# Latent attention's heads: rotation ahead of the norm, keys rotated once, and few-row products woven between the matmuls of gate chunks

## The chip, the cores and the metric

The kernel runs on one core of a Trainium2 chip. The metric is the device time in microseconds of one execution. TensorE (PE in the profile) multiplies, VectorE (DVE) and ScalarE (ACT) read its results from PSUM, GpSimd (POOL) does a few element-wise steps, and SyncE's queue (SP) loads the weights.

## The reference

Two transformer blocks of two layers each, all in float32, on 272 tokens (16 meta tokens and 256 others). The change is in the first block's latent attention, `mla`, which runs twice, once in each layer:

```
q = (rms_norm(c_q, q_a_g) @ w_uq).reshape(B, L, 8, 96)
kv = (rms_norm(c_kv, kv_a_g) @ w_ukv).reshape(B, L, 8, 128)
k_nope, v = kv[..., :64], kv[..., 64:]
k = concatenate([k_nope, broadcast(k_rope)], axis=-1)      # 64 + 32 = 96
q = rms_norm(q, q_norm_g);  k = rms_norm(k, k_norm_g)      # over the 96 of each head
q = concatenate([q[..., :64], apply_rope(q[..., 64:], cos, sin)], axis=-1)
k = concatenate([k[..., :64], apply_rope(k[..., 64:], cos, sin)], axis=-1)
o = causal_block_attention(q, k, v)
```

The last 32 rows of each key head are the same `k_rope` for all eight heads before the norm. The norm divides a head's 96 values at a token by one root, times a gain for each of the 96. `apply_rope` mixes row i with row i+16 of the 32, so it commutes with the division but not with the gain. The same layer has a gated recurrence (`hgrn2`) whose four heads are normed in the same way, and gates `sigmoid(h @ w_gate)` of 3 x 1024 columns.

## The kernel before, in words

Activations are held transposed: features on the 128 partitions, the 272 tokens along the free axis. Weights come as chunks of 128x1024 float32 (512 KB) through a ring of four slots that SP's queue fills in the order in which TensorE uses them. In the first block's projections TensorE uses a chunk as eight 128x128 weights against the activations (`project`); one float32 matmul is two instructions in the trace, here called passes.

PSUM has eight banks. `take` hands them out in strict rotation: each new product takes the next bank and waits until the engine that read the bank's result of eight takes ago has freed it. A product is therefore bound to the readers of the eight products before it.

The order of the work is a list of steps written out by hand (`schedule`). Each engine walks the same list and runs its own part of each step, if it has one; the instructions of one engine run in that order, so an engine stands still when the next step's input is late. Between engines there are semaphores and the banks.

The steps around the change, in each of the two layers, are these. `hgrn_values` makes the recurrence's outputs, `mla_up` multiplies up the queries (16 matmuls of 96 rows out), the keys (8 of 64 rows) and the values (3). Then there are three norms over heads, each in the same four parts: ACT squares the heads into the tile `SQ`; TensorE sums each head's rows with a matmul whose weight is a column of ones placed at the head's own output row (`row_sums`: 4 or 8 output rows); ACT takes the square root and DVE the reciprocal of these 4 or 8 rows (tile `HR`, part of `RS`; semaphore `row_roots`); TensorE spreads each row over 128 or 96 partitions with a matmul that has only 4 or 8 input rows (`spread`: one bank for each head), and DVE multiplies the head by it and by the gain. The three norms are that of the recurrence (`hgrn_norm`, `hgrn_spread`), of the queries (`head_norm`/`head_spread` with 0) and of the keys (with 1). After the heads' norm DVE rotates all eight heads' last 32 rows in four instructions: a shuffle, two products and a sum (`head_spread`). Between these steps stand six of the eight chunks of gate 2 (`gate(l, 2, m)`), which depend on nothing in them. After them comes the attention head by head.

HN is the normed input, CST the constants, MU and RS two scratch tiles, GATE the gates' tiles, and `region` holds all the rest, the heads among them.

Of the kernel before, what the change touches and what calls it, by code (L numbers as in the profile page):

```python
# [162 lines left out]
def parameters(i):  # L163
# [9 lines left out]
    col = lambda v: np.asarray(v).reshape(-1, 128).T  # L173
    for l in range(DEPTH):
# [7 lines left out]
        put(f"qn{l}", i["q_norm_g"][l][:, None])  # L182
        put(f"kn{l}", i["k_norm_g"][l][:, None])
# [8 lines left out]
        put(f"rbias{l}", np.concatenate([i["moe_br_g_2"][l], i["moe_br_e_2"][l].reshape(-1)])[None])  # L192
    put("ibias", i["ab_gate_b_2"][0, :4][:, None])
# [156 lines left out]
def build_program(nc, stream, params, consts, x_in, out, scratch):  # L350
    n_chunks = stream.shape[0] // 128
    with ExitStack() as ctx:
# [168 lines left out]
        def _(pe):  # L521
# [50 lines left out]
            def project(key, x, n=T, chunks=1, ready=None):  # L572

                dst, done = take(*key)
                for c in range(chunks):
# [129 lines left out]
            def row_sums(key, x, rows, heads):  # L705

                dst, done = take(*key)
                for h in range(heads):
                    mm(dst[:heads, :T], cst("pick", 15 - h, heads, rows), x(h), h == 0, h == heads - 1, done if h == heads - 1 else None)

# [5 lines left out]
            def hgrn_norm(l):  # L716
                pe.wait_ge(sem("hgrn_squares"), l + 1)
                row_sums(("hgrn_var", l), sq, 128, 4)

            def hgrn_spread(l):  # L720
                pe.wait_ge(sem("row_roots"), 3 * l + 1)
                for h in range(4):
                    spread(("hgrn_root", l, h), h, 128, 4)

# [6 lines left out]
            def mla_up(l):  # L731
                pe.wait_ge(sem("latents"), 2 * l + 1)
                for g in range(2):
                    w = chunk()
                    for h in range(4):
                        dst, done = take("q", l, 4 * g + h)
                        for k in range(2):
                            mm(dst[:QK, :T], w[:, 192 * h + 96 * k : 192 * h + 96 * k + 96], CQ[:, k, :], k == 0, k == 1, done if k else None)
                pe.wait_ge(sem("latents"), 2 * l + 2)
# [8 lines left out]
            def head_norm(l, which):  # L748
                pe.wait_ge(sem("head_squares"), 2 * l + which + 1)
                row_sums(("head_var", l, which), lambda h: SQ[:QK, T * h : T * h + T], QK, HEADS)  # L750

            def head_spread(l, which):
                pe.wait_ge(sem("row_roots"), 3 * l + 2 + which)
                for h in range(HEADS):
                    spread(("head_root", l, which, h), h, QK, HEADS)

            def att_scores(l, h):
                if h == 0:
                    pe.wait_ge(sem("heads_ready"), 2 * l + 2)
# [427 lines left out]
        def _(act):  # L1187
# [131 lines left out]
            def mla_up(l):  # L1319
                for h in range(HEADS):  # L1320
                    evacuate(("q", l, h), QH[:QK, h, :], rows=QK)
                fn(KH[NOPE:QK, :, :], bc(KR[NOPE:QK, None, :], [ROPE, HEADS, T]), ACT.Copy)
# [5 lines left out]
            def head_norm(l, which):  # L1328
# [3 lines left out]
                fn(SQ[:QK, : HEADS * T], src, ACT.Square, sem("head_squares"))  # L1332

# [253 lines left out]
        def _(dve):  # L1587
# [198 lines left out]

            def head_spread(l, which):
                x = (QH, KH)[which]
                for h in range(HEADS):
# [3 lines left out]

                r = slice(NOPE, QK)
                half = ROPE // 2
                shape = [ROPE, HEADS, T]
                c, s = CONSTS["cos"][0], CONSTS["sin"][0]
                lane(nc.vector.stream_shuffle(RSQ[r, :, :], x[r, :, :], [(i + half) % ROPE for i in range(ROPE)]))
                tt(RSQ[r, :, :], RSQ[r, :, :], bc(CST[r, None, s : s + T], shape), ALU.mult)
                tt(x[r, :, :], x[r, :, :], bc(CST[r, None, c : c + T], shape), ALU.mult)  # L1800
                tt(x[r, :, :], x[r, :, :], RSQ[r, :, :], ALU.add, sem("heads_ready"))
# [546 lines left out]
def schedule():  # L2348

    s = [("norm", 0), ("start",), ("store_bias",)]  # L2350
    for l in range(DEPTH):
# [68 lines left out]
```

## Time and profile before

| | us |
|---|---|
| median of three runs (lowest, highest) | 2438.68 (2435.79, 2441.68) |
| the profiled execution, whole | 2439.65 |
| its span, first to last instruction | 2437.9 |
| busy: PE, DVE, ACT, POOL | 2276.0, 1509.6, 1074.8, 240.7 |
| the stage of the change in layer 0: start of gate 2's chunk 0 to start of the first scores | 58.49 |
| the same in layer 1 | 57.84 |
| mean granted TensorE clock over the execution | 0.955 |

The granted clock is 1.00 at 2.4 GHz and 0.50 at 1.2 GHz; a number between is a mean over a stretch with both. A time in the tables of the trace is counted from the start of the span. A row's "x16" counts instructions, so that eight float32 matmuls are x16.

### The profile page before, as it was taken

Reading aid. Unit: us, or ns where it says so; the run is one execution under the profiler, and the core shown is the slowest. Engines: PE = TensorE matmul, PEld = TensorE weight load, DVE = VectorE, ACT = ScalarE, POOL = GpSimd, SP = SyncE. Lnnn points to the kernel's source line nnn. Section 1 sums busy time; section 2 is a strip of 40 time slices with the busy share of each in tenths; the row PEclk is TensorE's granted clock in tenths of the full one; section 3 lists DMA queues with packets and bytes.
Section 4 is the critical chain, followed back from the end, with each engine's and each line's share of the span. In section 5 each row is a group of like instructions: output and inputs, shape, how many; then the busy total and the mean of one; then the engine's idle time right before and its main releaser. Section 6 shows DMA issues by size and latency. Waiting matters only on the chain.

```text
span 2437.9 us, 36698 instructions
## 1 busy us (share of the span) xinstructions
PE 2276.0 (93%) x13888; PEld 1888.5 (77%) x13888; DVE 1509.6 (62%) x2343; ACT 1074.8 (44%) x1530; POOL 240.7 (10%) x241
## 2 busy tenths in 40 slices
PE   8999999999999999999999789999999787999997
PEld 6678567899867856889977379887888476988786
DVE  2846265656294626576534566888775166788876
ACT  1142432434114243244432345766654265567665
POOL 2814000101091400010100000000000000000000
PEclk9999799999999989999999689999999898999999
DMA  4332123455333212355542135888865413688884
GB/s 159 129 121 79 44 69 130 147 178 170 129 130 115 86 52 70 130 175 179 188 142 96 35 119 194 297 297 304 302 215 166 146 44 110 218 305 297 309 297 140
DMA packets 109808, 396.86 MB, mean 163 GB/s; under 512 B 12088, under 2 KB 14144, under 8 KB 109376
## 3 DMA queue, kind: packets, MB, share of 16 engines
q1 hardware_dynamic: 108576, 393.45, 47.9%
q8 instruction: 111, 1.82, 0.3%
q10 hardware_dynamic: 1056, 1.06, 0.1%
q14 instruction: 65, 0.53, 0.1%
HBM read 393.40 MB, written 1.06 MB: 162 GB/s over the span
## 4 chain that ended last, share of the span: by engine, by line
PE 76%; DVE 16%; ACT 4%; issue 2%; DMA 2%; SPq 0%; DVEq 0%; ACTq 0%
PE psum L536 75%; DVE W_LO L1593 3%; DVE region L1598 2%; PE psum L544 1%; DMA ring<-in_weights 1%; DVE region L1601 1%; ACT region L1201 1%; DVE RS L1630 1%; DVE region L1605 1%; ACT W_HI L1196 1%; DVE SQ L1598 1%; ACT SQ L1201 1%; ACT L1205 1%; DVE X_LO L1598 1%; ACT L1201 0%
## 5 line engine op out<-in xcount | busy, mean ns | idle before, releaser
L1593 DVE TENSOR_TENSOR W_LO<-ring,W_HI 128x1024 fp32r<-128x1024 f32 x434 | 531.8, 1225 | 219.1 <-ACT W_HI L1196 208.5
L1196 ACT ACTIVATE W_HI<-ring 128x1024 fp32r<-128x1024 f32 x434 | 460.8, 1062 | 339.1 <-PE psum L536 243.0
L536 PE MATMUL psum<-HN,ring 128*128 128x272 f32 (+1 forms) x1600 | 383.1, 400 | 12.2 <-DVE HN L1605 12.2
L536 PEld LDWEIGHTS psum<-HN,ring 128*128 128x128 f32 x1600 | 309.2, 195 | 80.7 <-issue 20.4
L536 PE MATMUL psum<-X_HI,W_HI 128*128 128x256 f32 x800 | 230.1, 288 | 12.5 <-DVE W_LO L1593 9.7
L536 PE MATMUL psum<-X_LO,W_HI 128*128 128x256 f32 x800 | 224.9, 281 | 0.0
L536 PE MATMUL psum<-X_HI,W_LO 128*128 128x256 f32 x800 | 224.7, 281 | 0.0
L1205 ACT ACTIVATE region<-psum 128x272 f32<-128x272 f32 (+9 forms) x227 | 89.5, 394 | 284.1 <-PE psum L536 264.5
L1593 DVE TENSOR_TENSOR W_LO<-SQ,W_HI 128x1024 fp32r<-128x1024 f32 x128 | 156.9, 1225 | 37.4 <-ACT W_HI L1196 32.9
L536 PE MATMUL psum<-FN_HI,W_HI 128*128 128x272 f32 (+1 forms) x592 | 169.8, 287 | 0.0
L536 PE MATMUL psum<-W_HI,XG_HI 128*128 128x512 f32 x384 | 152.9, 398 | 17.3 <-DVE W_LO L1593 15.3
L536 PE MATMUL psum<-FN_LO,W_HI 128*128 128x272 f32 (+1 forms) x592 | 168.5, 285 | 0.0
L536 PE MATMUL psum<-FN_HI,W_LO 128*128 128x272 f32 (+1 forms) x592 | 168.4, 284 | 0.0
L536 PEld LDWEIGHTS psum<-X_HI,W_HI 128*128 128x128 f32 x800 | 152.6, 191 | 18.8 <-issue 9.4
L1196 ACT ACTIVATE W_HI<-SQ 128x1024 fp32r<-128x1024 f32 x128 | 136.0, 1062 | 68.3 <-PE psum L536 65.8
L536 PE MATMUL psum<-region 128*32 128x4 f32 (+12 forms) x1360 | 150.3, 254 | 7.2 <-ACT region L1205 5.1
L536 PEld LDWEIGHTS psum<-X_LO,W_HI 128*128 128x128 f32 x800 | 152.5, 191 | 1.8
L536 PEld LDWEIGHTS psum<-X_HI,W_LO 128*128 128x128 f32 x800 | 153.0, 191 | 0.0
L536 PE MATMUL psum<-W_HI,XG_LO 128*128 128x512 f32 x384 | 151.0, 393 | 0.0
L536 PE MATMUL psum<-W_LO,XG_HI 128*128 128x512 f32 x384 | 150.6, 392 | 0.0
L536 PE MATMUL psum<-F_HI,W_HI 128*128 128x272 f32 (+1 forms) x512 | 145.7, 285 | 0.0
L536 PE MATMUL psum<-F_LO,W_HI 128*128 128x272 f32 (+1 forms) x512 | 144.6, 282 | 0.0
(306 smaller groups left out, 4273.9 us busy)
## 6 DMA issues: line engine op xcount, KB each, us to landing
ring<-in_weights SPq DMA_DIRECT2D x615, 512.0 KB, 4.2
SQ<-in_weights SPq DMA_DIRECT2D x128, 512.0 KB, 4.9
XT<-in_x SPq DMA_DIRECT2D x1, 1088.0 KB, 5.0
CST<-in_consts SPq DMA_DIRECT2D x1, 1082.5 KB, 7.2
SQ<-bias_by_distance ACTq DMA_DIRECT2D x1, 1024.0 KB, 5.4
out<-XT SPq DMA_DIRECT2D x8, 128.0 KB, 1.9
PAR<-in_params SPq DMA_DIRECT2D x1, 572.0 KB, 8.1
bias_by_distance<-MIX ACTq DMA_DIRECT2D x1, 12.0 KB
```

What stands on the lines that cost most here:

```text
L536: ins = nc.tensor.matmul(dst, w, x, start=start, stop=stop, skip_group_check=True)
L544: ins = nc.tensor.transpose(dst, src, ident(k))
L1196: lane(nc.scalar.activation(W_HI[:, s % SPLIT, :], ring_slot(n), ACT.Copy), split_hi)
L1201: lane(nc.scalar.activation(dst, src, f, **kw), sem_)
L1205: nc.scalar.activation(dst, src, f, **kw).then_inc(banks.freed(key), 1)
L1593: lane(nc.vector.tensor_tensor(W_LO[:, s % SPLIT, :], ring_slot(n), W_HI[:, s % SPLIT, :].bitcast(F32), ALU.subtract), split_lo)
L1598: lane(nc.vector.tensor_tensor(dst, a, b, op), done)
L1601: ins = nc.vector.tensor_scalar(dst, a, s1, s2, op0) if op1 is None else nc.vector.tensor_scalar(dst, a, s1, s2, op0, op1)
L1605: lane(nc.vector.scalar_tensor_tensor(dst, a, s, b, op0, op1), done)
L1630: lane(nc.vector.reciprocal(ap, ap))
```

## The change

The arithmetic is the same up to its order. These things change:

1. The rotation comes ahead of the norm. The gain of the 32 rotated rows goes into the rotation: one product takes the shuffled rows times the shuffled gain times the sine, another the rows times the gain times the cosine (`turn_queries`, `turned_queries`; `scalar_tensor_tensor` in place of `tensor_tensor`). The gain vectors of the norm have ones there. The squares are still taken of the unrotated rows, so ACT's squares come between.
2. The keys' 32 rows are rotated once, in the rope's own 32x272 tile (`hgrn_values` on DVE), and copied to the eight heads by ACT (`turned_key_rows`) after the squares; the copy of the unrotated rows (`key_rows`) stays, for the squares.
3. `mla_up` is cut into `mla_q` and `mla_kv`, with the recurrence's row sums (`hgrn_norm`) between them.
4. The spreads and the heads' row sums are no longer steps of their own on TensorE: `project` takes a generator (`beside`) and runs its products between the matmuls of a gate chunk. Chunk 0 holds the recurrence's 4 spreads and the queries' 8 row sums, chunk 2 five spreads of the queries, chunk 3 the other three and the keys' 8 row sums, chunk 5 six spreads of the keys; the last two stand behind it (`last_heads`). Chunks 1 and 4 are plain.
5. The first scores no longer wait for a whole stage of DVE (`heads_ready`): head h's scores wait until DVE has normed key head h.

The diff, cut to its core (`head_squares` and `turned_key_rows` are ACT's, the three below them DVE's):

```diff
-            def project(key, x, n=T, chunks=1, ready=None):
+            def project(key, x, n=T, chunks=1, ready=None, beside=None, count=0):
...
                         mm(dst[:, :n], columns(w, 128 * k, 128), x(8 * c + k), c + k == 0, last, done if last else None)
+                        while given < count * (k + 1) // KT:
+                            next(beside)
+                            given += 1
...
             def gate(l, b, m):
                 at = first_column(l)
-                project(("gate", l, b, m), lambda k: HN[:, k, at:], T - at)
+                count = {0: 12, 2: 5, 3: 11, 5: 6}.get(m, 0) if b == 2 else 0
+                project(("gate", l, b, m), lambda k: HN[:, k, at:], T - at, beside=beside_gate(l, m), count=count)
+
+            def beside_gate(l, m):
+                if m == 0:
+                    yield from hgrn_spreads(l)
+                    yield from head_norms(l, 0)
+                elif m == 2:
+                    yield from head_spreads(l, 0, 0, 5)
+                elif m == 3:
+                    yield from head_spreads(l, 0, 5, HEADS)
+                    yield from head_norms(l, 1)
+                elif m == 5:
+                    yield from head_spreads(l, 1, 0, 6)
...
             def att_scores(l, h):
-                if h == 0:
-                    pe.wait_ge(sem("heads_ready"), 2 * l + 2)
+                banks.await_read(pe, ("head_root", l, 1, h))
...
-            def head_norm(l, which):
+            def head_squares(l, which):
                 src = (QH, KH)[which][:QK, :, :].rearrange("p h t -> p (h t)")
                 if which:
                     wait_bank("head_var", l, 0)
                 fn(SQ[:QK, : HEADS * T], src, ACT.Square, sem("head_squares"))
+
+            def turned_key_rows(l):
+                act.wait_ge(sem("key_turned"), l + 1)
+                fn(KH[NOPE:QK, :, :], bc(MU[NOPE:QK, None, :T], [ROPE, HEADS, T]), ACT.Copy, sem("keys_turned"))
...
+            def hgrn_values(l):
+                r = slice(NOPE, QK)
+                banks.await_read(dve, ("rope", l))
+                lane(nc.vector.stream_shuffle(MU[r, :T], KR[r, :], half_turned))
+                stt(MU[r, :T], MU[r, :T], turn_gain(l, 1, 1), SIN, ALU.mult, ALU.mult)
+                stt(RS[r, :T], KR[r, :], turn_gain(l, 1, 0), COS, ALU.mult, ALU.mult)
+                tt(MU[r, :T], MU[r, :T], RS[r, :T], ALU.add, sem("key_turned"))
+
+            def turn_queries(l):
+                r = slice(NOPE, QK)
+                banks.await_read(dve, ("q", l, HEADS - 1))
+                lane(nc.vector.stream_shuffle(RSQ[r, :, :], QH[r, :, :], half_turned))
+                stt(RSQ[r, :, :], RSQ[r, :, :], turn_gain(l, 0, 1), bc(SIN[:, None, :], [ROPE, HEADS, T]), ALU.mult, ALU.mult)
+
+            def turned_queries(l):
+                r = slice(NOPE, QK)
+                dve.wait_ge(sem("head_squares"), 2 * l + 1)
+                stt(QH[r, :, :], QH[r, :, :], turn_gain(l, 0, 0), bc(COS[:, None, :], [ROPE, HEADS, T]), ALU.mult, ALU.mult)
+                tt(QH[r, :, :], QH[r, :, :], RSQ[r, :, :], ALU.add)
...
-        s += [("hgrn_values", l), ("mla_up", l), ("hgrn_norm", l), ("gate", l, 2, 0), ("hgrn_gates", l), ("hgrn_spread", l), ("head_norm", l, 0)]
-        s += [("gate", l, 2, 1), ("head_spread", l, 0), ("head_norm", l, 1), ("gate", l, 2, 2), ("head_spread", l, 1)]
-        s += [("gate", l, 2, m) for m in range(3, 6)] + [("att_scores", l, 0), ("att_scores", l, 1), ("gate", l, 2, 6), ("gate", l, 2, 7)]
+        s += [("hgrn_values", l), ("mla_q", l), ("hgrn_norm", l), ("turn_queries", l), ("mla_kv", l), ("head_squares", l, 0), ("key_rows", l)]
+        s += [("hgrn_spread", l), ("turned_queries", l), ("head_norm", l, 0), ("head_squares", l, 1), ("turned_key_rows", l)]
+        s += [("gate", l, 2, 0), ("hgrn_gates", l), ("gate", l, 2, 1), ("gate", l, 2, 2), ("head_spread", l, 0), ("head_norm", l, 1)]
+        s += [("gate", l, 2, 3), ("gate", l, 2, 4), ("gate", l, 2, 5), ("last_heads", l), ("head_spread", l, 1)]
+        s += [("att_scores", l, 0), ("att_scores", l, 1), ("gate", l, 2, 6), ("gate", l, 2, 7)]
```

TensorE's order in layer 0 before, from the last row sums of the recurrence to the first scores (HN,ring is a gate chunk, SQ,CST are row sums, RS,CST are spreads, region the scores; x8 counts matmuls):

```order
L536 MATMUL psum<-SQ,CST 4x272 x4
L536 MATMUL psum<-HN,ring 128x272 x8
L536 MATMUL psum<-RS,CST 128x272 x4
L536 MATMUL psum<-SQ,CST 8x272 x8
L536 MATMUL psum<-HN,ring 128x272 x8
L536 MATMUL psum<-RS,CST 96x272 x8
L536 MATMUL psum<-SQ,CST 8x272 x8
L536 MATMUL psum<-HN,ring 128x272 x8
L536 MATMUL psum<-RS,CST 96x272 x8
L536 MATMUL psum<-HN,ring 128x272 x24
L536 MATMUL psum<-region 128x128
```

The same place now, from the end of chunk 0 through the plain chunk 1 into chunk 2:

```order
L541 MATMUL psum<-SQ,CST 8x272
L541 MATMUL psum<-HN,ring 128x272
L541 MATMUL psum<-SQ,CST 8x272 x2
L541 MATMUL psum<-HN,ring 128x272 x10
L541 MATMUL psum<-RS,CST 96x272
L541 MATMUL psum<-HN,ring 128x272 x2
L541 MATMUL psum<-RS,CST 96x272
L541 MATMUL psum<-HN,ring 128x272
L541 MATMUL psum<-RS,CST 96x272
```

The groups of four and eight are gone; a spread or a row sum stands between single matmuls of a gate, and ten of the gate's own (chunk 1 and the first two of chunk 2) separate the queries' last row sum from their first spread.

ACT's order in layer 0 now, from the recurrence's root (RS<-psum 4x272) to the keys' root (the second RS<-psum 8x272):

```order
L1238 ACT_TABLE_LOAD
L1238 ACTIVATE RS<-psum,CST 4x272
L1238 ACTIVATE region<-psum 64x272 x8
L1238 ACTIVATE region<-psum 128x512 x2
L1238 ACTIVATE region<-psum 16x512
L1234 ACTIVATE SQ<-region 96x2176
L1234 ACTIVATE region<-region 32x2176
L1238 ACTIVATE RS<-psum,CST 8x272
L1234 ACTIVATE SQ<-region 96x2176
L1234 ACTIVATE region<-MU 32x2176
L1238 ACT_TABLE_LOAD
L1238 ACTIVATE GATE<-psum 128x272
```

Before, the first 8-row root and both squares stood behind the gate's sigmoids, each with a table load of its own around it; now both squares and the keys' two copies stand ahead of the sigmoid of gate 2's chunk 0.

## Rows read from the trace of the kernel before

**Rows 1.** The page: chain that ended last by engine; weight DMAs

```profile
PE 76%; DVE 16%; ACT 4%; issue 2%; DMA 2%; SPq 0%; DVEq 0%; ACTq 0%
...
ring<-in_weights SPq DMA_DIRECT2D x615, 512.0 KB, 4.2
```

**Rows 2.** Timeline of PE, layer 0: start us, us, engine, line, operation [idle before]

```profile
270.16 2.95 PE L536 MATMUL psum<-ring,region 128*128 128x512 f32 x6
...
274.87 3.93 PE L536 MATMUL psum<-HN,ring 128*128 128x272 f32 x16
278.79 2.09 PE L536 MATMUL psum<-RS,CST 4*128 4x272 f32 x8
284.75 7.01 PE L536 MATMUL psum<-SQ,CST 96*8 96x272 f32 x16 [3.86 <-ACT SQ L1201]
291.69 3.93 PE L536 MATMUL psum<-HN,ring 128*128 128x272 f32 x16
295.63 5.24 PE L536 MATMUL psum<-RS,CST 8*96 8x272 f32 x16
300.80 5.82 PE L536 MATMUL psum<-SQ,CST 96*8 96x272 f32 x16
306.55 3.94 PE L536 MATMUL psum<-HN,ring 128*128 128x272 f32 x16
313.41 5.94 PE L536 MATMUL psum<-RS,CST 8*96 8x272 f32 x16 [2.92 <-DVE RS L1785]
319.28 14.24 PE L536 MATMUL psum<-HN,ring 128*128 128x272 f32 x48
333.36 2.80 PE L536 MATMUL psum<-region 96*128 96x128 f32 x12
```

**Rows 3.** Windows: stretch, us, PE PEld DVE ACT POOL busy, granted clock, DMA

```profile
274.87:333.36 58.49, 51.70 (x169) 31.59 (x169) 36.87 (x37) 17.17 (x17) 0.00 (x0) 0.77 0.19 63
883.64:941.48 57.84, 51.69 (x169) 31.98 (x169) 36.84 (x37) 16.99 (x17) 0.00 (x0) 0.76 0.19 63
298.20:304.60 6.40, 6.40 (x15) 2.32 (x15) 5.32 (x8) 1.26 (x1) 0.00 (x0) 0.50 0.00 0
...
867.61:878.90 11.29, 11.29 (x49) 7.24 (x48) 0.00 (x0) 7.75 (x14) 0.00 (x0) 1.00 0.28 93
...
916.25:919.97 3.72, 3.72 (x17) 2.95 (x16) 3.69 (x2) 1.76 (x2) 0.00 (x0) 1.00 0.46 141
```

**Rows 4.** Timeline of ACT, layer 0

```profile
266.94 2.01 ACT L1201 ACTIVATE region<-region 32x2176 f32<-32x2176 f32 x1
268.98 5.22 ACT L1205 ACTIVATE region<-psum 64x272 f32<-64x272 f32 x11
...
276.32 0.48 ACT L1205 ACTIVATE RS<-psum,CST 4x272 f32<-4x272 f32 x1
278.91 1.28 ACT L1205 ACT_TABLE_LOAD   x1 [2.11 <-PE psum L536]
280.20 0.40 ACT L1205 ACTIVATE GATE<-psum 128x272 f32<-128x272 f32 x1
...
282.68 2.02 ACT L1201 ACTIVATE SQ<-region 96x2176 f32<-96x2176 f32 x1
```

**Rows 5.** Timeline of DVE, layer 0

```profile
279.62 0.44 DVE L1773 TENSOR_TENSOR region<-psum,region 128x272 f32<-128x272 f32 x1 [0.88 <-PE psum L536]
280.09 0.50 DVE L1605 SCALAR_TENSOR_TENSOR region<-region,PAR 128x272 f32<-128x272 f32 x1
...
301.54 2.58 DVE L1798 STREAM_SHUFFLE region<-region 32x2176 f32<-32x2176 f32 x1
...
309.06 2.42 DVE L1598 TENSOR_TENSOR region<-region 32x2176 f32<-32x2176 f32 x1
311.51 1.84 DVE L1785 RECIPROCAL RS<-RS 8x272 f32<-8x272 f32 x1
```

More of the change, by code:

```diff
@@ L173, in parameters @@
     col = lambda v: np.asarray(v).reshape(-1, 128).T
+    turns = [None, None]
     for l in range(DEPTH):
@@ L181, in parameters @@
         put(f"kva{l}", col(i["kv_a_norm_g"][l]))
-        put(f"qn{l}", i["q_norm_g"][l][:, None])
-        put(f"kn{l}", i["k_norm_g"][l][:, None])
+        for c, name in enumerate(("q", "k")):
+            g = np.asarray(i[f"{name}_norm_g"][l], np.float32)
+            put(f"{name}n{l}", np.concatenate([g[:NOPE], np.ones(ROPE)])[:, None])
+            turns[c] = g[NOPE:], np.roll(g[NOPE:], ROPE // 2)
         put(f"lb{l}", col(i["hgrn_lb_logits"][l]))
@@ L192, in parameters @@
         put(f"rbias{l}", np.concatenate([i["moe_br_g_2"][l], i["moe_br_e_2"][l].reshape(-1)])[None])
+        at = PARAMS[f"rbias{l}"][0]
+        out[NOPE:QK, at : at + 4] = np.stack([turns[0][0], turns[0][1], turns[1][0], turns[1][1]], axis=1)
     put("ibias", i["ab_gate_b_2"][0, :4][:, None])
@@ L668, in gate, with last_heads @@
                 at = first_column(l)
-                project(("gate", l, b, m), lambda k: HN[:, k, at:], T - at)
+                count = {0: 12, 2: 5, 3: 11, 5: 6}.get(m, 0) if b == 2 else 0
[11 more added lines that the diff above has]
+                    yield from head_spreads(l, 1, 0, 6)
+            def last_heads(l):
+                for _ in head_spreads(l, 1, 6, HEADS):
+                    pass
             def branch_out(l, b, c):
@@ L717, in hgrn_norm, with hgrn_spreads @@
                 pe.wait_ge(sem("hgrn_squares"), l + 1)
-                row_sums(("hgrn_var", l), sq, 128, 4)
-            def hgrn_spread(l):
+                for _ in row_sums(("hgrn_var", l), sq, 128, 4):
+                    pass
+            def hgrn_spreads(l):
                 pe.wait_ge(sem("row_roots"), 3 * l + 1)
@@ L723, in hgrn_spread @@
                     spread(("hgrn_root", l, h), h, 128, 4)
+                    yield
             def mla_norm(l):
@@ L729, in mla_norm, with mla_q @@
                 column_sums(("ckv_var", l), lambda k: sq(6), 1, T)
-            def mla_up(l):
+            def mla_q(l):
                 pe.wait_ge(sem("latents"), 2 * l + 1)
@@ L746, in mla_up, with head_norms, head_spreads @@
                     mm(dst[:n, :], CKV[:, lo : lo + n], w[:, 512:1024], done=done)
-            def head_norm(l, which):
+            def head_norms(l, which):
                 pe.wait_ge(sem("head_squares"), 2 * l + which + 1)
[L750 to L754, printed above, removed]
+                yield from row_sums(("head_var", l, which), lambda h: SQ[:QK, T * h : T * h + T], QK, HEADS)
+            def head_spreads(l, which, lo, hi):
+                if lo == 0:
+                    pe.wait_ge(sem("row_roots"), 3 * l + 2 + which)
+                for h in range(lo, hi):
                     spread(("head_root", l, which, h), h, QK, HEADS)
+                    yield
             def att_scores(l, h):
-                if h == 0:
-                    pe.wait_ge(sem("heads_ready"), 2 * l + 2)
+                banks.await_read(pe, ("head_root", l, 1, h))
                 for i, (lo, n) in enumerate(TOK1):
@@ L1317, in mla_norm, with mla_q, mla_kv @@
                 root(("ckv_var", l), MU[:, :T], T, 128)
-            def mla_up(l):
+            def mla_q(l):
                 for h in range(HEADS):
                     evacuate(("q", l, h), QH[:QK, h, :], rows=QK)
-                fn(KH[NOPE:QK, :, :], bc(KR[NOPE:QK, None, :], [ROPE, HEADS, T]), ACT.Copy)
+            def mla_kv(l):
                 for h in range(HEADS):
@@ L1332, in head_norm, with key_rows @@
                 fn(SQ[:QK, : HEADS * T], src, ACT.Square, sem("head_squares"))
+            def key_rows(l):
+                fn(KH[NOPE:QK, :, :], bc(KR[NOPE:QK, None, :], [ROPE, HEADS, T]), ACT.Copy)
+            def turned_key_rows(l):
+                act.wait_ge(sem("key_turned"), l + 1)
+                fn(KH[NOPE:QK, :, :], bc(MU[NOPE:QK, None, :T], [ROPE, HEADS, T]), ACT.Copy, sem("keys_turned"))
+            def head_norm(l, which):
                 wait_bank(*(("head_root", l, 0, HEADS - 1) if which else ("hgrn_root", l, 3)))
@@ L1785, in head_norm, with turn_gain @@
                 lane(nc.vector.reciprocal(HR[:HEADS, :], HR[:HEADS, :]), sem("row_roots"))
+            def turn_gain(l, which, shuffled):
+                at = PARAMS[f"rbias{l}"][0] + 2 * which + shuffled
+                return PAR[NOPE:QK, at : at + 1]
+            half_turned = [(i + ROPE // 2) % ROPE for i in range(ROPE)]
+            COS, SIN = (CST[NOPE:QK, CONSTS[n][0] : CONSTS[n][0] + T] for n in ("cos", "sin"))
+            def hgrn_values(l):
[15 more added lines that the diff above has]
+                tt(QH[r, :, :], QH[r, :, :], RSQ[r, :, :], ALU.add)
             def head_spread(l, which):
                 x = (QH, KH)[which]
+                if which:
+                    dve.wait_ge(sem("keys_turned"), l + 1)
                 for h in range(HEADS):
@@ L1792, in head_spread @@
                     free(ins, "head_root", l, which, h)
[L1794 to L1801, printed above, removed]
             def att_scores(l, h):
```

4 lines of the change are left out of this document (3 added, 1 removed).

## The prediction

> **What bounds the kernel now.** I read the chain of waits first: three quarters of it is TensorE at work [rows 1]. A microsecond taken from TensorE's own path is a microsecond of the end, and ring and DMA are no other bound here. Then I read TensorE's timeline through the stage that the change touches, from gate 2's chunk 0 to the first scores, once in each layer [rows 2], and then the same stretches as windows with the granted clock [rows 3]. Three things are to be seen there.
>
> The stage takes 58.49 us in layer 0 and 57.84 in layer 1 [rows 3]. TensorE is busy for 51.70 and 51.69 of these, so it stands idle for 6.79 and 6.15 us. In layer 0 that is 3.86 us ahead of the queries' row sums, which wait for ACT's squares, and 2.92 ahead of the keys' spreads, which wait for a reciprocal that DVE reaches only after the queries' rotation [rows 2].
>
> The work is slower than it need be. A gate chunk takes 3.93 us in one place (16 passes, 0.246 each), but the three plain ones at 319.28 take 14.24 in place of 11.8. Eight row sums take 7.01 and 5.82, eight spreads 5.24 and 5.94 [rows 2]. In layer 1, 48 passes of the up-projection with 96 and 64 rows out run at clock 1.00 in 11.29 us, 0.235 each [rows 3], so 16 passes could take 3.8.
>
> The cause is the clock: its mean over the stage is 0.77 and 0.76 [rows 3]. In layer 0 it falls to 1.2 GHz in the middle of the queries' spreads, with TensorE never idle: from 298.20 to 304.60 TensorE is busy for all 6.40 us at 0.50 [rows 3]. What the engine did before it fell was a gate chunk and some 2.5 us of products with only eight input rows; it came back in the middle of the row sums, which have 96 input rows. So here the spreads, though busy, are what loses the clock, and gates or row sums are what gets it back.
>
> The Trainium skill ("TensorE: Matmul & The Clock Gate", part 1 on the clock gate) ties the clock to how busy TensorE is and warns of idle gaps. The 6.40 busy microseconds at 0.50 [rows 3] speak against that as the whole rule. By the page alone weaving would give back no clock, since the products keep TensorE just as busy where they stand now; that result is the second rival below.
>
> **The change part by part.** TensorE does the same 168 passes in the stage: 96 of six gate chunks, 8 of the recurrence's spreads, 64 of heads' row sums and spreads. The recurrence's row sums only change places with the keys and values ahead of the stage, so the stage starts at the same time.
>
> *The passes at 2.4 GHz.* Layer 0: 6 x 3.93 = 23.58 for gates, 2.09 for the recurrence's spreads [rows 2], 64 x 0.235 = 15.04; together 40.7. Layer 1 has 256 columns in gates: 6 x 3.72 = 22.32 [rows 3], together 39.45. No row shows single few-row passes between single gate passes. If the exchange costs TensorE nothing, 40.7 stands; the upper bound would be a small gap at each change of kind. The recurrence's four spreads, each with its own bank and wait, ran at 0.26 a pass against 0.235 for longer runs [rows 2, 3], and 0.025 on 72 passes is 1.8 us a layer. I take nothing, as 16 passes of a gate directly behind other work show no gap.
>
> *The waits that go.* Count from the start of chunk 0. The recurrence's row sums now end before keys (8 matmuls, 16 x 0.235 = 3.8) and values (2.95, rows 2), that is 6.7 us before. ACT's table load and root take 1.28 + 0.48, DVE's reciprocal 1.84 [rows 4, 5], so the recurrence's roots are there at -3.1, and TensorE asks at +0.5. ACT then moves keys and values (5.22) and squares the queries (2.02, rows 4): -4.9 + 7.2 = +2.3. TensorE asks for the squares after four gate matmuls and four spreads, 1.96 + 2.09 = +4.05. Both waits are covered, with 3.6 and 1.7 us to spare.
>
> *The wait that comes.* Banks go round in eights. Chunk 0 takes one, then four spreads, one row-sum bank, chunk 1, chunk 2: the queries' first spread in chunk 2 is the ninth and needs the bank of chunk 0, which ACT frees with the gate's sigmoid. From the end of the queries' row sums ACT has the root 0.48, the keys' squares 2.02, the copy of the turned rows 2.01, a table load 1.28 and the sigmoid 0.40 [rows 4]: 6.2, with hand-over 6.3. TensorE has chunk 1 and two matmuls of chunk 2: 3.93 + 0.98 = 4.9 in layer 0, 3.72 + 0.93 = 4.65 in layer 1. New waits: 1.4 and 1.65 us. Behind the waiting spread stand the other six matmuls of chunk 2 and everything after.
>
> By the Trainium skill ("ScalarE: Activation LUTs", What ACT_TABLE_LOAD costs) a switch of tables costs a drain of about 1.38 us on top of the load; the sigmoid here starts 0.01 us after the load's 1.28 [rows 4], so the row decides. With the page's drain this wait would be 1.4 us longer in each layer, 2.8 in all.
>
> DVE is no later: from the roots at -3.1 + 0 it shuffles and multiplies the queries (2.58 + about 2.5) until +2.1, waits for the recurrence's spreads, multiplies 4 x (0.44 + 0.50) until about +6.2, finishes the rotation (2.5 + 2.42) at +11.2 and, with the row sums done at 3.93 + 2.09 + 3.76 = +9.8, gives the reciprocal at +13.1 [rows 5]. TensorE asks at +14.7, the bank comes at +16.1. That a 32x2176 product with a gain costs about what one without does (2.42) is an estimate; 0.50 against 0.44 on 272 columns [rows 5] bounds it by 2.75, which the 3 us to the bank hold.
>
> *The keys.* Their squares are done 2.5 us after the queries' sums and are asked for over 10 later. After their row sums (end of chunk 3) ACT has load and root (1.76) and DVE the reciprocal (1.84): 3.6, against chunk 4 and one matmul of chunk 5, 4.4: covered by 0.8, in layer 1 by 0.6. The rotation of all key heads (2.58 + three products of about 2.43, 9.9 us of DVE) becomes four instructions on 272 columns; before, it was hidden under the three gates [rows 2], so its removal is worth nothing directly. ACT's copy of 2.01 is the price, and it is in the wait above. The first scores ask for one key head; DVE norms a head in 0.5 us, at the pace of the spreads.
>
> *Weights.* A chunk lands 4.2 us after issue [rows 1]; a woven chunk takes over 6 us and a plain one 3.9 with three others ahead in the ring. No new wait.
>
> *The clock.* In the new order full-row work is everywhere between spreads, but not by much: in chunk 2 there are 5 x 0.47 = 2.35 us of spreads beside 3.93 of gate and the new wait of 1.4; around the end of chunk 5 eight spreads (3.8) beside 3.93. No row shows such a mixture. From below, the clock stays at 2.4 GHz: cost 0. From above, both places lose it as the spreads did: the spreads of rows 2 were 1.4 and 2.1 us over 3.8, the row sums behind 2.0 over, the three gates behind 2.4, so a fall costs 3.4 to 4.5, and two of them about 8 a layer. I take one fall a layer, 4 us, the middle.
>
> *Sum.* Layer 0: 40.7 + 1.4 + 4 = 46.1, a gain of 58.49 - 46.1 = 12.4. Layer 1: 39.45 + 1.65 + 4 = 45.1, a gain of 12.7. Together 25.1 us. The attention that follows is unchanged and starts earlier; nothing later is bound by a fixed time. The profiled execution took 2439.65, so 2414.6; it lies 1 us above the median of the runs, so 2414 in round numbers.
>
> **Rivals.** *A, full clock.* As above with no fall: 58.49 - 42.1 = 16.4 and 57.84 - 41.1 = 16.7, together 33: 2406 to 2407, less 1 against the median. For it: every gate chunk that stands between two few-row groups runs at its full 3.93 [rows 2], so gate work holds the clock. Against it: in chunk 2 the new wait and the spreads come together.
>
> *B, only the waits.* The few-row passes and the gates beside them run at the mean pace they have now, 51.7 us in both layers, and only idle time changes: 6.79 - 1.4 and 6.15 - 1.65, together 9.9: 2430, 2429 against the median. For it: 51.7 twice, in two different places of the program. Against: the long groups of spreads that came before each fall are gone.
>
> *C, the clock is lost for the whole stage.* With a spread every second or third matmul TensorE may never do enough full work to get the clock back once it is gone. At 1.2 GHz 16 passes take 7.01 [rows 2], 0.44 each: 168 x 0.44 = 73.9 against 58.49, and 57.84, that is 31 us slower: 2470. It decides where over half of the passes are slow: the stage now spends 58.49 / 168 = 0.348 a pass, between 0.242 and 0.44, so slower from 54% on. Against it: row sums brought the clock back at 304.6, and chunks 1 and 4 are plain.
>
> *D, the weave stands still.* Every woven product holds the gate's matmuls behind it. If one of the covered waits (1.7 us at the squares, 0.6 to 0.8 at the keys' roots) is missed in each chunk by as much as it has now, TensorE is idle for as long as before and the falls stay: no change, 2438.
>
> **How the numbers follow.** Forecast, about one fall a layer: 0.48, 2414. A: 0.27. B: 0.15. C: 0.04. D: 0.06. The range reaches down to A with the 1 us of the median and a little more, 2404, and up into B, 2427. No change means within 0.2%, about 5 us, which is what three runs can tell. Faster 0.91 (forecast, A, B and a part of D), within 0.2% 0.05, slower 0.04 (C).
>
> **What would show it.** Right: the stage, gate 2's chunk 0 to the first scores, takes 42 to 48 us in both layers, its mean clock is 0.85 or more, and TensorE's longest idle time in it is 1.2 to 2 us at the first spread of chunk 2, behind ACT's gate sigmoid. No wait stands at chunk 0's spreads or row sums nor at chunk 5. Wrong in the clock: passes woven in chunks 2, 3 or 5 at 0.44, a mean clock under 0.80. Wrong in the waits: idle time in chunk 0 or 5, or DVE as the releaser in chunk 2. And wrong in the whole: attention's first part, or the recurrence ahead, longer by what the stage gained.

## The result and the profile after

| | before | after |
|---|---|---|
| median (lowest to highest) | 2440.18 (2435.79 to 2443.39), 4 runs | 2463.79 (2455.31 to 2473.70), 4 runs |
| ratio to before, 95% interval | | 1.0107 [1.0079, 1.0135] |
| the profiled execution, whole | 2439.65 | 2459.64 |
| stage of the change, layer 0 | 58.49 | 69.80 |
| stage of the change, layer 1 | 57.84 | 62.61 |

The changed kernel is 1.1% slower, where 1% faster was forecast. First the windows of the changed kernel: the two stages (they answer to the first two of [rows 3]), then two stretches inside them (us, busy PE PEld DVE ACT POOL, granted clock, DMA).

```profile
274.68:344.48 69.80, 68.04 (x170) 29.20 (x169) 22.18 (x28) 17.85 (x17) 0.00 (x0) 0.69 0.16 53
902.15:964.76 62.61, 60.59 (x169) 27.36 (x168) 21.86 (x28) 17.66 (x17) 0.00 (x0) 0.75 0.18 59
...
300.80:324.70 23.90, 23.90 (x44) 8.32 (x44) 2.96 (x6) 0.40 (x1) 0.00 (x0) 0.51 0.06 22
921.90:952.80 30.90, 30.90 (x59) 11.14 (x59) 3.45 (x7) 2.04 (x4) 0.00 (x0) 0.51 0.05 17
```

The idle time has gone, as intended: 1.76 and 2.02 us are left of 6.79 and 6.15. What went up is TensorE's busy time for the same passes, 51.7 to 68.0 and 60.6 us. The mean clock is 0.69 and 0.75, under the 0.77 and 0.76 of before. The last two rows say that TensorE can be busy for every microsecond of 24 and of 31 and still run at 1.2 GHz.

The timeline of TensorE in layer 0 answers to [rows 2].

```profile
274.68 0.73 PE L541 MATMUL psum<-HN,ring 128*128 128x272 f32 x2
275.33 0.72 PE L541 MATMUL psum<-RS,CST 4*128 4x272 f32 x2
275.98 0.73 PE L541 MATMUL psum<-HN,ring 128*128 128x272 f32 x2
276.64 1.18 PE L541 MATMUL psum<-RS,CST 4*128 4x272 f32 x4
...
291.17 4.85 PE L541 MATMUL psum<-HN,ring 128*128 128x272 f32 x20
297.79 0.66 PE L541 MATMUL psum<-RS,CST 8*96 8x272 f32 x2 [1.76 <-ACT GATE L1238]
...
306.58 1.22 PE L541 MATMUL psum<-RS,CST 8*96 8x272 f32 x2
307.73 1.28 PE L541 MATMUL psum<-HN,ring 128*128 128x272 f32 x2
308.94 1.22 PE L541 MATMUL psum<-RS,CST 8*96 8x272 f32 x2
...
332.14 0.73 PE L541 MATMUL psum<-HN,ring 128*128 128x272 f32 x2
...
333.42 0.73 PE L541 MATMUL psum<-HN,ring 128*128 128x272 f32 x2
...
344.48 5.27 PE L541 MATMUL psum<-region 96*128 96x128 f32 x12
349.68 8.60 PE L541 MATMUL psum<-HN,ring 128*128 128x272 f32 x32
```

Read starts, since the ends of matmuls overlap. At the full clock a gate matmul (x2) between spreads takes 275.33 - 274.68 = 0.65 us; sixteen passes in 3.93 are 0.49 for one matmul [rows 2], and that row holds the two ends of its block (e2 will show 0.46 without them). Two spreads in a row take 1.11 (276.64 to 277.75), so the second adds only 0.46, although it too has a bank of its own: the gap comes with the change of kind, not with each product. The row of weight loads says what the gap is:

```profile
275.33 0.29 PEld L541 LDWEIGHTS psum<-RS,CST 4*128 4x128 f32 x2 [0.36 <-issue]
275.98 0.30 PEld L541 LDWEIGHTS psum<-HN,ring 128*128 128x128 f32 x2 [0.36 <-issue]
```

The loads of a new kind start together with its first matmul (275.33 and 275.98 in both timelines), 0.36 us after the last load: none is laid beside the matmul ahead. A pair of a gate matmul and a spread takes 1.28 us at the full clock (332.14 to 333.42) and 2.36 at the low one (306.58 to 308.94). The clock is low from 280 to 290.7, from 300.8 to 324.7 and from 334.8 to 351.8 (windows of 0.52, 0.51 and 0.50); the last of these also slows the first scores (5.27 against 2.80) and the two gate chunks behind them (8.60 against 7.60).

The two stages lost 11.31 and 4.77 us and what stands behind the first one 3.5: 19.6 of the 20.0 between the profiled executions.

### The profile page after: what moved, and what is told of

Its sections match the earlier page's. It is cut to its first block, busy times and chain, and to the rows that moved or that the text cites. A ratio compares the mean times of both kernels' runs of the same rounds, so it can differ in the third digit from the quotient of the medians.

```text
span 2457.8 us, 36718 instructions
## 1 busy us (share of the span) xinstructions
PE 2306.3 (94%) x13888; PEld 1886.3 (77%) x13888; DVE 1494.5 (61%) x2343; ACT 1074.0 (44%) x1528; POOL 240.3 (10%) x241
## 4 chain that ended last, share of the span: by engine, by line
PE 78%; DVE 15%; ACT 4%; issue 2%; DMA 1%; DVEq 0%; ACTq 0%; SPq 0%
PE psum L541 76%; DVE W_LO L1636 3%; DVE region L1641 1%; PE psum L549 1%; DVE region L1644 1%; ACT region L1234 1%; DVE RS L1673 1%; DVE region L1648 1%; DVE X_LO L1641 1%; DVE SQ L1641 1%; ACT SQ L1234 1%; ACT W_HI L1229 1%; ACT L1238 0%; ACT L1234 0%; DMA ring<-in_weights 0%
## 5 line engine op out<-in xcount | busy, mean ns | idle before, releaser
L541 PE MATMUL psum<-HN,ring 128*128 128x272 f32 (+1 forms) x1600 | 407.6, 411 | 12.2 <-DVE HN L1648 12.2
L541 PEld LDWEIGHTS psum<-region 128*32 128x32 f32 (+6 forms) x1360 | 107.8, 144 | 50.1 <-issue 26.4
```

The lines of the kernel that those rows point to most:

```text
L541: ins = nc.tensor.matmul(dst, w, x, start=start, stop=stop, skip_group_check=True)
```

## Experiments

Two explanations stood at the start. *S, the change of shape*: each exchange between a gate's 128x128 weight and a few-row one costs a gap. *W, the wait*: the new wait in chunk 2 is what takes the clock. For the low clock itself a third: *F, the few-row spreads*, with 4 or 8 input rows, take it, waits or not. Beside them the kernel before was timed again: its medians were 2437.58 (beside e1 to e4), 2438.24 (e5 to e8) and 2438.25 (e9 to e12). Ratios therefore compare better across these groups than medians do.

| kernel | median us | ratio to before |
|---|---|---|
| changed kernel | 2463.79 | 1.0107 [1.0079, 1.0135] |
| e1, products in blocks | 2417.61 | 0.9925 [0.9897, 0.9953] |
| e2, woven, spreads of full shape | 2411.42 | 0.9901 [0.9869, 0.9933] |
| e3, woven, all of full shape | 2429.75 | 0.9968 [0.9948, 0.9988] |
| e4, before with spreads of full shape | 2434.70 | 0.9994 [0.9977, 1.0010] |
| e5, the wait hidden | 2457.97 | 1.0077 [1.0052, 1.0101] |
| e6, blocks and spreads of full shape | 2401.25 | 0.9849 [0.9827, 0.9870] |

**e1, blocks instead of the weave.** The same steps, banks and order of steps; a chunk's few-row products stand in one block behind its eight gate matmuls.

```diff
-                        while given < count * (k + 1) // KT:
-                            next(beside)
-                            given += 1
+                for _ in range(count):
+                    next(beside)
```

> The changed kernel, but each gate chunk's few-row products stand behind its eight matmuls and not between them; the rotation, the cut of the up-projection and the order of all else stay. Theory S (two costs of weaving: each change between a gate matmul and a few-row product exposes a weight load, 0.15 us at 2.4 GHz and 0.3 at 1.2, and the clock, once lost, does not come back among them): the changes of kind fall from some 40 to 8 in a layer, the stage from 69.8 and 62.6 us to about 52, total about 2427. Rival W (the new wait at the bank of chunk 0 and the longer chain through ACT are the cost): the weave is innocent, the total stays near 2460.

Measured 2417.61, under the 2427 expected. Windows of e1's stages and its timeline in layer 0:

```profile
276.49:319.54 43.05, 43.05 (x170) 27.68 (x169) 22.14 (x28) 17.86 (x17) 0.00 (x0) 0.93 0.26 86
875.20:914.33 39.13, 39.13 (x169) 26.85 (x169) 21.71 (x28) 17.79 (x18) 0.00 (x0) 1.00 0.28 94
```

```profile
282.38 5.52 PE L541 MATMUL psum<-SQ,CST 96*8 96x272 f32 x16
...
314.52 5.09 PE L541 MATMUL psum<-RS,CST 8*96 8x272 f32 x16
319.54 5.27 PE L541 MATMUL psum<-region 96*128 96x128 f32 x12
```

TensorE is never idle, since the block comes late enough for the bank. Layer 1 runs at 1.00 and takes 39.13 us. So the weave itself, not the rest of the change, made it slow. The clock still falls in layer 0, in row sums behind spreads and at the last spreads, and it is low in the first scores of both layers (5.27 and 5.22 in place of 2.80).

**e2, spreads of full shape, still woven.** The 4 or 8 input rows become 128; the added ones are multiplied by zero. The heads' spreads also get 128 output columns in place of 96.

```diff
-                mm(dst[:rows, :T], ident(heads)[:, row : row + 1].to_broadcast([heads, rows]), HR[:heads, :], done=done)
+                mm(dst[:, :T], ident(128)[:, row : row + 1].to_broadcast([128, 128]), RS[:, :T], done=done)
```

> The changed kernel, woven as it is, but every spread reads 128 rows (weight: 128x128 from the identity, zero against all rows but one) and writes 128, so that its shape is a gate matmul's; the row sums keep 96 rows in and 8 out. Theory S, in the form that the shape is what costs: no gap at spreads, still 0.15 us at each change to and from the row sums, and the clock no longer falls at the spreads: stage about 46, total about 2415. Rival B (the gap belongs to the change of PSUM bank, whatever the shape): a gate matmul beside a spread still takes 0.65 us, total above 2430. Rival R (only the share of input rows counts for the clock, nothing for the gap): gap 0.65, clock 1.00, total about 2425.

Measured 2411.42, with both waits still there. Windows of the stages, then TensorE's timeline in layer 0:

```profile
274.79:318.64 43.85, 42.09 (x169) 26.99 (x169) 21.70 (x28) 17.85 (x17) 0.00 (x0) 1.00 0.25 84
870.40:915.30 44.90, 42.88 (x170) 28.14 (x169) 22.14 (x29) 17.92 (x18) 0.00 (x0) 0.96 0.25 82
```

```profile
275.81 0.62 PE L541 MATMUL psum<-HN,ring 128*128 128x272 f32 x2
276.27 1.08 PE L541 MATMUL psum<-RS,CST 128*128 128x272 f32 x4
277.19 0.62 PE L541 MATMUL psum<-HN,ring 128*128 128x272 f32 x2
...
283.76 0.73 PE L541 MATMUL psum<-HN,ring 128*128 128x272 f32 x2
284.42 1.08 PE L541 MATMUL psum<-SQ,CST 96*8 96x272 f32 x4
...
292.05 0.70 PE L541 MATMUL psum<-RS,CST 128*128 128x272 f32 x2 [1.76 <-ACT GATE L1238]
```

```profile
275.58 0.42 PEld L541 LDWEIGHTS psum<-HN,ring 128*128 128x128 f32 x2
```

Between full-shape products a step is 0.46 us and the gap is gone: the weight of the gate matmul at 275.81 is loaded from 275.58 (last row, weight loads), ahead of its start. At the row sums, which keep 8 output columns, a gate matmul still takes 0.66. The clock is 1.00 through all of layer 0, with a wait of 1.76 in its middle, and the long low stretches are gone from layer 1 too. W is right only in small: after layer 1's wait of 2.02 the clock is low for about 3 us (0.54 from 888 to 891) and then comes back, in the same weave. In chunk 0 the two kernels differ in nothing but the spreads' input rows, and there the changed kernel lost its clock at 280. It did so in layer 0 only: in layer 1 the same chunk ran at 1.00. The mean clock of each whole run says the same as the profiles: 0.963 to 0.967 in the four runs of e2, 0.942 to 0.951 in the four of the changed kernel. The row sums woven among gates (96 input rows) do not take the clock here, although the gap stands at them. That speaks for F, and against the gaps or few output columns as what takes it. e4 parts F from the gaps once more, since inside its blocks there is no gap to remove.

**e3, the row sums too.** Their weight comes from a new table of constants, a one in column 15 of 143.

```diff
+    put("wide", np.tile(np.eye(143)[15], (96, 1)))
...
-                    mm(dst[:heads, :T], cst("pick", 15 - h, heads, rows), x(h), ...)
+                    mm(dst[:, :T], cst("wide", 15 - h, 128), x(h), ...)
```

> As the woven kernel with 128-row spreads, and the heads' row sums have full weights too (128 rows, of which 96 are not zero, by 128 columns), so that every product in the stage has the shape of a gate matmul. Theory S: no gap anywhere, 168 passes of 0.246 us and the one wait: stage 43 in layer 0, 41.5 in layer 1, total about 2408. Rival B: the gaps stay, 0.65 us for a single gate matmul, total above 2430.

The gaps are gone, as S says. Timeline of TensorE in layer 1, whose stage starts at 876.90; its only wait, then the first scores:

```profile
892.65 0.70 PE L542 MATMUL psum<-RS,CST 128*128 128x272 f32 x2 [2.22 <-ACT GATE L1242]
...
916.68 2.80 PE L542 MATMUL psum<-region 96*128 96x128 f32 x12
```

The stage takes 39.78 us at a clock of 1.00, of which the passes are 37.56. Layer 0 takes 42.49 with 40.53 busy, but its clock is low for some 3 us after the wait of 1.96 (0.54 from 291.3 to 294.9). In layer 1 no low clock followed a longer wait, 2.22. So what a wait of about 2 us does to the clock is not settled by its length in these runs. The whole got slower than e2 all the same, 2429.75 where 2408 was expected. The loss is spread over the program outside the stage; e7 to e12 follow it.

**e4, the kernel before with e2's edit alone.**

> The kernel before, with nothing changed but the spreads, which read and write 128 rows. Theory S: the clock no longer falls in the spreads, but it still falls at the idle time ahead of the queries' row sums, and all waits stay: stage about 50, total 2439 - 15 = about 2424. Rival: the number of input rows has nothing to do with the clock, it falls as before, and wider weights cost a little: 2440 to 2445.

A miss. Timeline of e4 in layer 0:

```profile
295.13 3.93 PE L536 MATMUL psum<-RS,CST 128*128 128x272 f32 x16
299.02 3.83 PE L536 MATMUL psum<-SQ,CST 96*8 96x272 f32 x16
...
312.08 6.70 PE L536 MATMUL psum<-RS,CST 128*128 128x272 f32 x16 [5.36 <-DVE RS L1785]
```

The same block of sixteen passes, with no gap inside it before or now, no longer takes the clock, and the row sums behind it keep it (3.93 and 3.83 against 5.24 and 5.82 in [rows 2]): F holds. But TensorE only arrives earlier at the reciprocal behind DVE's rotation: the wait grew from 2.92 to 5.36, the clock fell in it (0.81 from 309 to 312), and the time is that of before within its interval. The stage took 54.99, not 50.

**e5, the wait hidden.** Woven with the shapes of the changed kernel, but the five spreads of chunk 2 begin in its second half.

```diff
+                        share = max(k - 3, 0) / 4 if count == 5 else (k + 1) / KT
-                        while given < count * (k + 1) // KT:
+                        while given < int(count * share):
```

> The woven kernel with one edit: the five spreads of a chunk that has five start in its second half (none beside k = 0 to 3), so that ACT's gate sigmoid is over when the first of them asks for a bank; all shapes are as in the changed kernel. If the wait of 1.8 to 2.0 us in the third chunk is what loses the clock: no wait longer than 0.5 us there, the second layer's mean clock back near 1.00, its stage at 46 to 50 us where the changed kernel has 62.6. If it is the mixture of few-row products among gate matmuls that doesn't keep the clock (rival): the wait goes, the clock falls at the same place or a chunk later, and the second layer's stage stays at 57 to 62 us; the whole within 8 us of the changed kernel's 2464.

The wait is 0.40 us in layer 0. In chunk 0 of layer 0 the clock held this time. In chunk 2 it falls all the same, after five microseconds of mixture (timelines of both layers):

```profile
294.57 0.66 PE L541 MATMUL psum<-RS,CST 8*96 8x272 f32 x2 [0.40 <-ACT GATE L1239]
...
299.46 1.22 PE L541 MATMUL psum<-HN,ring 128*128 128x272 f32 x2
...
900.37 0.66 PE L541 MATMUL psum<-RS,CST 4*128 4x272 f32 x1
900.95 1.22 PE L541 MATMUL psum<-HN,ring 128*128 128x256 f32 x2
```

In layer 1 it fell in chunk 0, where TensorE had waited for nothing. That stage takes 61.81 us at 0.72 (896.36 to 958.17). As the cause of the long low stretches W is out. Hiding the wait was worth 6 us of medians, of which the waits are 3.4; the intervals of the two ratios overlap. The few-row weave lost its clock in every stage of the two kernels that have it, but not at the same place: first in chunk 0 of layer 0 and in chunk 2 of layer 1 in the changed kernel, and the other way round in e5. What decides between them was not found.

**e6, both edits that helped.**

> The changed kernel with both edits that helped singly: the products of a chunk as one block behind its gate matmuls, and the spreads as full 128 by 128 products. If the two losses (the change of shape at each exchange, and few-row products that leave the clock low) are separate and nothing else changes: stages of 41 to 43 us in both layers, few changes of shape left, the whole at 2404 to 2410, under each of the two alone (2417.6 and 2411.4). If woven full-row spreads had already taken all there was (rival): no better than 2411, within 0.2%.

```profile
279.31:318.51 39.20, 39.20 (x170) 28.50 (x170) 21.43 (x27) 17.86 (x17) 0.00 (x0) 1.00 0.28 94
870.67:908.59 37.92, 37.92 (x170) 28.50 (x170) 21.45 (x27) 17.68 (x17) 0.00 (x0) 1.00 0.29 97
```

The stages, 39.20 and 37.92 us, and the whole are below what was expected. Both run without idle time at 1.00, and the first scores behind layer 0 take 2.80 again. With 2401.25 it beats both kernels: 1.5% under before and, by the ratios, 2.6% under the changed one. All of the change but the weave is in it. Its gain over e4 is 33 us for the same spreads. The new order of rotation and norms and the place of the blocks have it between them; e4's idle time is what they remove, but no run parts them.

**e7 and e8, the table.** e7 is e3 with a table of 160 columns. e8 is e2 with the table of 143 loaded and used by nothing.

> Woven with all side products in full 128 by 128 shape, as in the run of 2429.75, but the added table of constants has 160 columns (640 bytes a partition) in place of 143 (572). If the loss of that run outside the stage (its later stages each ran a little longer) comes from where the wider table pushes the buffers behind it: 2408 to 2413, the late row sums at 0.46 us each. If it comes from the row sums' shape or from the table's load: 2427 to 2432 again.

> The version with full-row spreads alone (2411.42) and an unused table of constants of 143 columns in front of the buffers; every instruction is the same. If the place of the buffers is the cause: 2426 to 2432. If the shape of the row sums is: 2409 to 2414.

e7 2426.75, ratio 0.9968 [0.9947, 0.9989]; e8 2435.40, ratio 0.9988 [0.9970, 1.0006]. An unused table costs 24 us by the medians and 21 by the ratios: the row sums' shape is not to blame for e3. It is more than the 2426 to 2432 expected for the place. A width of 640 bytes does not mend it; e7 alone, inside neither range but next to the second, would have pointed at the wrong cause.

**e9 and e10, which side of the shape.** Row sums with 128 input rows and 8 columns, and with 96 rows and 128 columns.

> Woven, spreads as full products; the row sums read all 128 rows (the added ones times zero) but still have 8 output columns. It asks which side of the shape makes the weight load wait for the matmul before it. If the count of rows decides: a row sum among gate matmuls goes from 0.55 us at the full clock to 0.44 to 0.47, as in the run with both sides full. If the count of columns decides (rival): it stays at 0.55 and the gate matmul behind it at 0.65. The whole time says nothing here, since the added table alone costs 24 us.

> The other half: row sums of 96 rows with 128 output columns. If the count of rows decides: row sums stay at 0.55 us and the gate matmul behind them at 0.65. If the count of columns decides: both are at 0.44 to 0.49.

One run each, 2435.17 and 2426.73. Timeline of e9, then of e10:

```profile
281.31 0.72 PE L542 MATMUL psum<-HN,ring 128*128 128x272 f32 x2
281.96 1.08 PE L542 MATMUL psum<-SQ,CST 128*8 128x272 f32 x4
282.98 0.73 PE L542 MATMUL psum<-HN,ring 128*128 128x272 f32 x2
```

```profile
280.57 0.62 PE L542 MATMUL psum<-HN,ring 128*128 128x272 f32 x2
281.03 1.08 PE L542 MATMUL psum<-SQ,CST 96*128 96x272 f32 x4
281.95 0.62 PE L542 MATMUL psum<-HN,ring 128*128 128x272 f32 x2
```

With 8 columns the gate matmul still takes 0.65 start to start; with 128 columns and 96 rows it takes 0.46. Here the columns decide. The spreads of the changed kernel have 128 columns in chunk 0 and only 4 rows, and have the gap too; so few rows bring it as well, and 96 are not few. Where between 4 and 96, and between 8 and 128, the bound lies was not tried.

**e11 and e12, where the table's cost comes from.** e2 with 572 bytes left empty behind the constants on the chip, and e2 with the input in device memory 143 columns wider but the same columns loaded.

> The version with full-row spreads (2411.42) and 572 unused bytes a partition behind the constants in on-chip memory; nothing more is loaded, and the input in device memory is as it was. If the place of the buffers on the chip cost the 24 us of the run with the unused table: 2430 to 2438. If it was the longer constants input, which moves what lies behind it in device memory: 2409 to 2414.

> The version with full-row spreads (2411.42) and the constants input 143 columns wider in device memory, of which the same columns as before are loaded into the same place. If device memory's layout cost the 24 us: 2430 to 2438. If the place of the buffers on the chip did: 2409 to 2414.

e11 2432.28, ratio 0.9984 [0.9968, 1.0000]; e12 2414.30, ratio 0.9902 [0.9876, 0.9927]. The place of the buffers behind CST is the cause (18 us between the two), the input is not. Most frequent matmuls on the page of e2, then of e11 (busy us, mean ns):

```profile
L541 PE MATMUL psum<-X_LO,W_HI 128*128 128x256 f32 x800 | 226.8, 283 | 0.0
L541 PE MATMUL psum<-FN_LO,W_HI 128*128 128x272 f32 (+1 forms) x592 | 168.5, 285 | 0.0
```

```profile
L542 PE MATMUL psum<-X_LO,W_HI 128*128 128x256 f32 x800 | 229.0, 286 | 0.0
L542 PE MATMUL psum<-FN_LO,W_HI 128*128 128x272 f32 (+1 forms) x592 | 169.9, 287 | 0.0
```

The same matmuls take about 1% longer, in one execution of each. These two groups make 3.6 us of it; TensorE's busy time as a whole went from 2259.3 to 2280.3, and no other group of one shape grew by more than 2.8. What in the place does it stays open; in e7 these rows are as in e2 and the time is not. Between before and the changed kernel nothing was moved (X_LO,W_HI has 281 and 282 ns), so this has no part in the result.

## Why the prediction was wrong

The stages in the prediction's own terms, with the changes of kind as a term of their own. The waits are read in the changed kernel; passes and changes of kind are estimates from e3's and its own rows, as said below, and the low clock is what is left of the stage:

| us | layer 0, predicted | measured | layer 1, predicted | measured |
|---|---|---|---|---|
| passes at 2.4 GHz | 40.7 | 38.8 | 39.45 | 37.6 |
| changes of kind | 0 | 8.7 | 0 | 8.7 |
| the new wait | 1.4 | 1.76 | 1.65 | 2.02 |
| low clock | 4 | 20.5 | 4 | 14.3 |
| stage | 46.1 | 69.80 | 45.1 | 62.61 |

*The passes.* Nearly right, some 1.9 us too high in each layer. In e3's layer 1, with no change of kind and the full clock, they took 37.56. Layer 0 has 272 columns in gates where layer 1 has 256, which adds 6 x (3.93 - 3.72) = 1.26: 38.8. The prediction's 3.93 for a gate chunk is that of a block between few-row groups, so it holds the changes at its two ends. The trace of before has two chunks in a row, which take less than twice 3.93:

```profile
336.09 7.60 PE L536 MATMUL psum<-HN,ring 128*128 128x272 f32 x32
```

*"If the exchange costs TensorE nothing, 40.7 stands ... I take nothing."* This step failed. In layer 1 chunk 0 ran woven at the full clock throughout, from 902.15 to 913.75: 11.60 us against 9.06 for the same products in full shape (e3, 876.90 to 885.96), so 2.54 for its 16 changes of kind, 0.16 each. A stage has 55 of them: 8.7 us. e1's layer 1 bears it out: 37.56 and ten changes of 0.16 are 39.2, and it took 39.13. The bound of 1.8 was wrong as well, since it went by 0.025 a pass from the recurrence's eight spreads. That row held the answer: 2.09 in place of eight times 0.235 is 0.21 more in a block with one change at each end. It was spread over the passes instead of being charged to the change, and sixteen passes of a gate were taken as proof of no gap where they pay for just the ends of one block.

*"I take one fall a layer, 4 us, the middle."* This failed by more. The clock gives the last row of the table by another way: a mean of 0.69 is 62% of 69.80 at the low level, 43.3 us, and a pair that takes 2.36 there and 1.28 at the full clock loses 0.46 of each such microsecond: 19.9. In layer 1 it is 50%, 31.3 us, 14.4. The upper bound of 8 was built from falls that each ended within a chunk or two, since behind each stood a long run of gates or row sums. In the weave no such run follows; once low, the clock stayed low through the mixture, and came back in the last row sums (324.5) and in the plain chunk 4 (952.8). Rival C was this mechanism (31 us, given 0.04); its argument that every second or third product would be a spread was right, and its counter-argument, that row sums brought the clock back, held for a block of sixteen passes and not for row sums with gates of slow pace between: from 280 to 290.7 there is no spread, and the clock stayed low for 10.7 us. It decided from 54% of slow passes; 62% and 50% of the time were low, and the gaps did the rest.

*Busy and slow.* To the 6.40 busy microseconds at 0.50 [rows 3] the changed kernel adds 30.90 busy ones at 0.51. The Trainium skill ("TensorE: Matmul & The Clock Gate", part 1 on the clock gate) ties the clock to how busy the engine has been; as the whole rule these rows speak against it. In e4 the clock did fall in an idle gap, of 5.36 us, and there the trace agrees with the page of the Trainium skill.

*The waits.* Right, all of them. Neither chunk 0 nor chunk 5 has one; the new one stands at the first spread of chunk 2, is released by ACT's gate sigmoid, and is 1.76 and 2.02 us long. ACT's chain there, 0.48, 2.02, 2.01, 1.28 and 0.40, is as priced:

```profile
291.36 0.48 ACT L1238 ACTIVATE RS<-psum,CST 8x272 f32<-8x272 f32 x1 [11.84 <-PE psum L541]
291.87 2.02 ACT L1234 ACTIVATE SQ<-region 96x2176 f32<-96x2176 f32 x1
293.92 2.01 ACT L1234 ACTIVATE region<-MU 32x2176 f32<-32x2176 f32 x1
295.95 1.28 ACT L1238 ACT_TABLE_LOAD   x1
297.25 0.40 ACT L1238 ACTIVATE GATE<-psum 128x272 f32<-128x272 f32 x1
```

The table load starts 0.02 us after the copy ahead of it and the sigmoid 0.02 us after the load. The Trainium skill ("ScalarE: Activation LUTs", What ACT_TABLE_LOAD costs) adds a drain of about 1.38 us to each switch of tables, which these rows do not show. DVE is never the releaser, and the ring is never late. The signs named for "wrong in the clock" (passes at 0.44 in chunks 2, 3 or 5, a mean under 0.80) are those that came.

The whole change except its weave was thus worth 20 us (e1), near the 25 forecast, but by other terms: e1 has no wait where 3.05 us were forecast, ten changes of kind in a layer, and a low clock that reaches into the first scores. The weave cost 46 us on top of e1 (2463.79 - 2417.61; 44 by the ratios).

## What to carry to other kernels

Few-row or few-column products are not free filler between full matmuls: put them in blocks, where each block pays for the change of shape at its two ends and no more, and give them full shape if the zeros cost nothing. A price of a few tenths that a row shows at the edge of a block belongs to the edge; before weaving, multiply it by the number of edges. For a stretch at the low clock ask not only what takes the clock but what stands behind it to give it back, since that sets how long it lasts.

## What the runs showed of the hardware

- A change between a 128x128 weight and one of 4 or 8 input rows or 8 output columns cost 0.16 us on average at the full clock (11.60 against 9.06 us for 16 changes); with 96 rows and 128 columns there was none (e10, 0.46 us a matmul).
- Spreads of 4 or 8 input rows took the clock while TensorE was busy (30.90 us at 0.51), though not every time that the same chunk ran; of 128 rows, in the same places, they did not.
- Of four waits of about 2 us in full-row weaves, two were followed by some 3 us of low clock (2.02 in e2, 1.96 in e3) and two were not (1.76 in e2, 2.22 in e3).
- 572 empty bytes a partition behind the constants cost 18 us in 2414 (e11 against e12), with 283 (e2) going to 286 ns (e11) in the most frequent matmul. An effect as large as the change under study can come from where a buffer lies, so an experiment that adds a buffer needs a run with the buffer alone.
